# A second, transposed copy of x for the first norm, and a new order of the first loads, in a two-block transformer kernel on one Trainium2 core

## The reference

```
def rmsnorm(x, g):
    xf = x.astype(jnp.float32)
    y = xf * lax.rsqrt(jnp.mean(xf * xf, axis=-1, keepdims=True) + EPS)
    return (y * g.astype(jnp.float32)).astype(x.dtype)
```

## Time and profile before

| what | value |
|---|---|
| median of 3 runs | 866.22 us (866.06 to 866.31) |
| span of the profiled execution | 864.7 us |
| around it, to the median | 1.5 us |
| TensorE busy | 856.5 us, 99% of the span |
| VectorE, ScalarE busy | 604.2 us (70%), 501.3 us (58%) |
| HBM read | 152.53 MB |

### The profile page before, as it was taken

The page is one execution under the profiler, slowest core; times in us unless marked ns, Lnnn a source line. Parts: engine busy times, 40 slices in busy tenths (PEclk is TensorE's granted clock), DMA queues, the critical chain, the costliest instruction groups (busy, mean ns, idle before and its releaser), DMA issues.

```text
span 864.7 us, 12203 instructions
## 1 busy us (share of the span) xinstructions
PE 856.5 (99%) x4654; PEld 733.2 (85%) x4654; DVE 604.2 (70%) x1068; ACT 501.3 (58%) x873; POOL 36.1 (4%) x49
## 2 busy tenths in 40 slices
PE   9999999999999999999999999999999999999996
PEld 8998888888889999978888788888888888888885
DVE  6986666655767885779687466788458566777584
ACT  6435545446655676968678457654535456766540
POOL 0000000000010000000000001100020000000002
PEclk9999999999999999999999999999999999999999
DMA  9864544652583877543332457573764555434421
GB/s 326 280 222 166 195 149 144 207 194 98 195 268 128 285 241 233 148 147 98 127 119 97 146 194 225 191 269 126 265 202 153 182 195 192 150 120 172 165 79 49
DMA packets 86808, 154.36 MB, mean 179 GB/s; under 512 B 3744, under 2 KB 24352, under 8 KB 86752
## 3 DMA queue, kind: packets, MB, share of 16 engines
q1 hardware_dynamic: 85248, 149.19, 51.3%
q0 software_dynamic: 1360, 4.33, 1.7%
q10 hardware_dynamic: 144, 0.07, 0.0%
HBM read 152.53 MB, written 1.05 MB: 178 GB/s over the span
## 4 chain that ended last, share of the span: by engine, by line
PE 97%; DVE 1%; DMA 0%; ACT 0%; POOL 0%; issue 0%; DVEq 0%; POOLq 0%
PE acc L2273 11%; PE acc L2275 11%; PE acc L2274 11%; PE acc L2247 9%; PE acc L2249 9%; PE acc L2248 9%; PE acc L2291 5%; PE acc L2285 4%; PE acc L2286 4%; PE acc L2287 4%; PE acc L2292 3%; PE misc L2315 2%; PE misc L2445 2%; PE misc L2434 1%; PE acc L2305 1%; PE misc L2487 1%
## 5 line engine op out<-in xcount | busy, mean ns | idle before, releaser
L1455 DVE TENSOR_TENSOR wboth<-raw,wboth 128x1024 fp32r<-128x1024 f32 (+1 forms) x280 | 326.4, 1214 | 60.5 <-ACT wboth L973 59.0
L973 ACT ACTIVATE wboth<-raw 128x1024 fp32r<-128x1024 f32 (+1 forms) x280 | 278.9, 1052 | 122.9 <-PE acc L2275 67.4
L2273 PE MATMUL acc<-wboth,xhiA 128*128 128x512 f32 x272 | 107.8, 396 | 0.0
L2275 PE MATMUL acc<-wboth,xloA 128*128 128x512 f32 x272 | 106.1, 390 | 0.0
L2274 PE MATMUL acc<-wboth,xhiA 128*128 128x512 f32 x272 | 106.1, 390 | 0.0
L2247 PE MATMUL acc<-wboth,xhiA 128*128 128x512 f32 x240 | 93.9, 391 | 0.0
L2249 PE MATMUL acc<-wboth,xloA 128*128 128x512 f32 x240 | 93.5, 390 | 0.0
L2248 PE MATMUL acc<-wboth,xhiA 128*128 128x512 f32 x240 | 93.4, 389 | 0.0
L2291 PE MATMUL acc<-xC,wboth 128*128 128x512 f32 x192 | 68.7, 399 | 0.0
L2273 PEld LDWEIGHTS acc<-wboth,xhiA 128*128 128x128 f32 x272 | 51.1, 188 | 11.4 <-issue 1.2
L2275 PEld LDWEIGHTS acc<-wboth,xloA 128*128 128x128 f32 x272 | 51.0, 188 | 10.9
(11 more groups left out here) (335 smaller groups left out, 1721.0 us busy)
## 6 DMA issues: line engine op xcount, KB each, us to landing
raw<-in_w_in_dram SPq DMA_DIRECT2D x36, 1024.0 KB, 5.2
raw<-in_ret_w_in_dram SPq DMA_DIRECT2D x22, 1024.0 KB, 5.6
raw<-in_nsa_w_in_dram SPq DMA_DIRECT2D x16, 1024.0 KB, 5.5
raw<-in_kv_w_dram SPq DMA_DIRECT2D x12, 1024.0 KB, 6.7
raw<-in_ret_w_out_dram SPq DMA_DIRECT2D x8, 1024.0 KB, 5.1
raw<-in_ple_w_gate_dram SPq DMA_DIRECT2D x8, 1024.0 KB, 5.1
raw<-in_nsa_w_out_dram SPq DMA_DIRECT2D x8, 1024.0 KB, 5.1
raw<-in_cmp_w_k_dram SPq DMA_DIRECT2D x4, 1024.0 KB, 5.5
```

Source lines behind the costliest of these rows:

```text
L973: nc.scalar.activation(to_hi, src, ACT.Copy).then_inc(hi_done, 1)
L1455: nc.vector.tensor_tensor(to_lo, src, to_hi.bitcast(F32), ALU.subtract).then_inc(lo_done, 1)
L2273: nc.tensor.matmul(o, xh, hi[:, j, off:off + cols], start=start, stop=False)
L2275: ins = nc.tensor.matmul(o, xl, hi[:, j, off:off + cols], start=False, stop=stop)
```

## The change

x is handed in a second time as `x_T`, of shape 128 x 8 x 256 (column within the k-tile, k-tile, row), arranged on the host. It is loaded in four pieces, k-tiles 0, 1, 2 to 3 and 4 to 7, the second by SP behind chunk 0 and the others by ScalarE's queue; it lies in a part of the arena that was empty. ScalarE and VectorE read it there, in place of PSUM. The transposes go. `head` is loaded in two parts, the gains behind the first piece of x_T, and the identity last. The rows of x, which the squares and the residual sums still need, are loaded by SP behind chunk 4 and ahead of chunk 5. ScalarE squares all four pieces ahead of its high half of chunk 5, VectorE makes the low half of chunk 5 ahead of both sums, and the product `roots` stands behind all of chunk 5 instead of in its middle.

```
+XT_CUTS = (0, 1, 2, 4, 8)
...
-    norm("ret")
     r("ret_q0")
-    plan.half("ret_k0", 0, 0)
+    r("ret_k0", [0])
     m("roots")
-    plan.half("ret_k0", 0, 1)
     r("ret_k0", [1])
...
+        x_T = k3("x_T", 2048, KD)
...
+        def xT_part(i):
+
+            return x_T[:, XT_CUTS[i]:XT_CUTS[i + 1]], w["x_T"][:, XT_CUTS[i]:XT_CUTS[i + 1]]
+
+        def xT_wait(eng, k):
+
+            if k in XT_CUTS:
+                eng.wait_ge(xT_in[XT_CUTS.index(k)], 16)
...
         def _(sp):
-            for m in range(MT):
-                sp.dma_start(h[:, m], w["x"][0, m * P:m * P + P]).then_inc(x_in[m], 16)
             for c, (key, src, ks, width, *_) in enumerate(plan.chunks):
...
+                if c == 5:
+                    for m in range(MT):
+                        sp.dma_start(h[:, m], w["x"][0, m * P:m * P + P]).then_inc(x_in[m], 16)
                 sp.dma_start(raw_part(c).rearrange("p (k n) -> p k n", n=width), src).then_inc(raw_sem(c), 16)
+                if c == 0:
+                    sp.dma_start(*xT_part(1)).then_inc(xT_in[1], 16)
...
             def first_norm_hi():
 
+                act.wait_ge(ret_gain_in, 16)
                 for k in range(KD):
-                    misc_wait(act, "norm", "ret", k % 4)
-                    if k >= 4:
-
-                        act.wait_ge(operand_ready, xt_no["norm", "ret", k - 4] + 1)
-                    nc.scalar.activation(xhi["A"][:, k], first_columns(k), ACT.Copy, scale=cv["ret"][:, k:k + 1])                        .then_inc(operand_hi_done, 1)
+                    xT_wait(act, k)
+                    nc.scalar.activation(xhi["A"][:, k], x_T[:, k], ACT.Copy, scale=cv["ret"][:, k:k + 1])\
+                        .then_inc(operand_hi_done, 1)
...
-            act.dma_start(head[:], w["head"]).then_inc(head_in, 16)
+            act.dma_start(*xT_part(0)).then_inc(xT_in[0], 16)
+            act.dma_start(head[:, P:], w["head"][:, P:]).then_inc(ret_gain_in, 16)
             act.wait_ge(warm_set, 1)
             nc.scalar.activation(ssq[:, 0, 0:1], gains[:, 0, 0:1], ACT.Copy)
-            act.wait_ge(head_in, 16)
+            act.dma_start(*xT_part(2)).then_inc(xT_in[2], 16)
+            act.dma_start(*xT_part(3)).then_inc(xT_in[3], 16)
+            act.dma_start(head[:, 0:P], w["head"][:, 0:P]).then_inc(head_in, 16)
             first_norm_hi()
             for m in range(MT):
                 act.wait_ge(x_in[m], 16)
                 for nb in range(2):
                     square(m, nb)
-                split_until(len(FIRST_CUTS) + m)
+            split_until(len(FIRST_CUTS) + 1)
...
             first_norm_lo()
+            split_until(len(FIRST_CUTS))
             norm_stats("ret", 0)
-            split_until(len(FIRST_CUTS))
             asked = norm_stats("ret", 1)
 
             dve.wait_ge(*asked)
+            dve.wait_ge(head_in, 16)
...
                 elif kind == "roots":
 
+                    pe.wait_ge(head_in, 16)
                     pe.wait_ge(roots_spread, 1)
...
+    args["x_T"] = give("x_T", _np.ascontiguousarray(
+        _np.asarray(inputs["x"])[0].reshape(T, KD, P).transpose(2, 1, 0)))
```

More of the change, by code:

```diff
@@ L577, in build @@
         ret_kT = k3("ret_kT", 2048, 8)
-        here[0] += 2048
+        x_T = k3("x_T", 2048, KD)
         sTd = [carve(f"sTd{i}", 384) for i in range(2)]
@@ L673, in build @@
         head_in = sem("head_in")
+        ret_gain_in = sem("ret_gain_in")
+        xT_in = [sem(f"xT_in{i}") for i in range(len(XT_CUTS) - 1)]
         trig_in = sem("trig_in")
@@ L809, in build @@
         ones = gains[:, 0, 0:P]
-        def first_columns(k):
-            at_ = k // 4 * T
-            return bank("norm", "ret", k % 4)[:, at_:at_ + T]
+        def xT_part(i):
[3 more added lines that the diff above has]
+                eng.wait_ge(xT_in[XT_CUTS.index(k)], 16)
         def scores_of(hd, mp, qt):
@@ L1501, in first_norm_lo @@
                     dve.wait_ge(operand_hi_done, xts[0])
-                    freed[("norm", "ret", k % 4)] = xt_on(nc.vector.scalar_tensor_tensor(
-                        out=xlo["A"][:, k], in0=first_columns(k),
+                    xt_on(nc.vector.scalar_tensor_tensor(
+                        out=xlo["A"][:, k], in0=x_T[:, k],
                         scalar=cv["ret"][:, k:k + 1], in1=xhi["A"][:, k].bitcast(F32), op0=ALU.mult, op1=ALU.subtract))
@@ L2327, in misc @@
                     j = name[2]
[L2328 to L2338, removed]
-                    else:
[L2340 to L2344, removed]
-                            pe.wait_ge(residual_piece, 4 * (NORMS.index(name[1]) - 1) + MT * (1 + j // 2))
-                            parts = [(h[:, m, k * P:k * P + P], P) for k in (2 * j, 2 * j + 1) for m in range(MT)]
-                        ins = transposes(ps, parts)
+                    if name[1] == "kv":
+                        m, k0 = divmod(KD // 2 * j, KD)
+                        pe.wait_ge(rows_normed, m + 1)
+                        parts = [(xn_kv[:, m, k * P:k * P + P], P) for k in range(k0, k0 + KD // 2)]
+                    else:
+                        pe.wait_ge(residual_piece, 4 * (NORMS.index(name[1]) - 1) + MT * (1 + j // 2))
+                        parts = [(h[:, m, k * P:k * P + P], P) for k in (2 * j, 2 * j + 1) for m in range(MT)]
+                    ins = transposes(ps, parts)
                 elif kind == "roots":
+                    pe.wait_ge(head_in, 16)
                     pe.wait_ge(roots_spread, 1)
```

## The result

| | before | after |
|---|---|---|
| median | 866.27 us (866.06 to 866.59, 6 runs) | 869.15 us (868.52 to 869.98, 6 runs) |
| span of the profiled execution | 864.7 us | 867.0 us |
| start of `ret_q0`, first product | 8.09 | 6.37 |
| start of `ret_k0` | 19.70 | 20.72 |
| start of `ret_q1` | 31.64 | 33.85 |

The account below looks back on a forecast made before the run. TensorE, busy 99% of the span, bounds the kernel. The 2.3 us won in front go to waiting for chunk 5 (`ret_k0` at 19.6); plus 13.03, `ret_q1` starts at 32.63 against 31.46: +1.2, so 867.4 us, range 865.7 to 868.7.

Parts of the forecast that it names:

- The first wait: TensorE ahead of `ret_k0`: idle 1 to 1.5 us for VectorE's low half of chunk 5, spending the 2.3 us won.
- The first product: Start of `ret_q0`: without transposes it begins at 5.75, 2.3 us earlier, with x_T and gains landing at 4.7.
- The megabyte of part 2: Loads ahead of chunk 5: x_T adds 1.049 MB, 2.66 us at 394 GB/s, so chunk 5 lands at 17.2, not 14.5.
- A wait for x_T against weights may add some tenths: Products of `ret_q0`: x_T and weights share the DMA engines, which may delay its end by some tenths.
- S: Start of `ret_k0`: forecast 19.6 against 19.70 before, with a range from 18.6 to 20.7.
- part 3: Roots behind chunk 5: `ret_q1` starts at S + 13.03, where TensorE alone would be ready at S + 11.76; wait 1.27 us.
- The squares: ScalarE ahead of chunk 5: four squares, 2.9 us in all, cost nothing, covered with about 1 us to spare.
- Rival B, the clock: `ret_q0` without transposes: the clock rises late; a rise at 13 gives S = 20.9 and 868.7 us; chance 0.12.
- Rival D: Ahead of `ret_q1`: the roots wait does not decide, S = 19.6, start at 31.36, 866.1 us; chance 0.08.
- Rivals C and E: Front: C, chunk 5 isn't late, 865.9 us, chance 0.16; E, neither wait binds, clock high at once, 863.8, chance 0.05.

Follow-up runs that it names:

- d1: Changed kernel with the last piece of x_T issued by SyncE behind chunk 2 instead of by ScalarE ahead of it; 869.35 us, ratio 1.0034.
- p2: Changed kernel with the four x_T pieces as arrays of their own, all issued by SyncE ahead of their chunks; 868.96 us, ratio 1.0032.
- b1: Kernel before plus x_T loaded in one 1 MB transfer ahead of chunk 5, read by nothing; 866.49 us, ratio 1.0001.
- w1: Changed kernel with six ones products ahead of `ret_q0` in place of four; 869.64 us, ratio 1.0038.
- r1: Changed kernel with the product `roots` back in the middle of chunk 5's products; 868.41 us, ratio 1.0025.
- e1: Changed kernel with x_T loaded by SyncE in one transfer of 8 KB rows ahead of chunk 0; 869.37 us, ratio 1.0030.
- e3: e1 with eight ones products instead of four and nothing else changed; 867.27 us, ratio 1.0012.
- r2: Kernel before with only the product `roots` moved behind all of chunk 5's products; 867.44 us, ratio 1.0013.
- p1: Changed kernel with each of the four x_T pieces as its own array in HBM, same order and queues; 868.52 us, ratio 1.0026.
- q1: Changed kernel with all four x_T pieces issued by SyncE, each ahead of its chunk, instead of three by ScalarE; 869.90 us, ratio 1.0040.
- b3: Kernel before with x loaded in four 256 KB transfers of 2 KB runs instead of two of 512 KB; 867.53 us, ratio 1.0016.
- x1: Changed kernel with the rows of x loaded behind chunk 5 and squared behind its high half; 869.10 us, ratio 1.0031.
- x2: Changed kernel with both load orders altered, x1 and d1 together; 867.57 us, ratio 1.0014.

## Why the prediction was wrong

**Sign and mechanism, half right.** I forecast that the gain in front would be spent waiting for chunk 5, and that the roots would add a wait; the likeliest time was slower by 1.2 us. Both waits are there. Measured is 2.9, and the range ended at 868.7. The first wait does not show as idle time in after: TensorE was still in `ret_q0`, held back by the low clock until 12.5, when chunk 5's low half became ready, and the 1 to 1.5 us of idleness that I forecast ahead of `ret_k0` appear only in d1 (1.34) and p2 (1.41).

**The first product**: forecast 5.75, measured 6.37. ScalarE waited for the gains until 5.29, not 4.7; by my own bounds (4.3 to 5.1) this was late by 0.2. It had no consequence.

**The megabyte of part 2** is the step that failed. I put x_T at 394 GB/s, the rate of 9 to 14 us, and gave the start of the transfers half a microsecond in the bound only. b1 shows that 2.66 us is right for this megabyte in one transfer; cut in pieces of 1, 2 and 4 KB runs and placed first, it slowed all transfers between 2 and 7 us to 249 GB/s, and chunk 5 landed at 18.3, 3.8 us later than before and at the far end of my range. "A wait for x_T against weights may add some tenths" was the same error at chunk 2: it was 1.6 us in w1. By the sum of part 3, S = 20.72 instead of 19.6 gives 20.72 + 13.03 = 33.75, and measured is 33.85.

**The squares** ("cost nothing, covered by chunk 5's own transfer with about 1 us to spare") were a second term that failed. They took 3.0 us, about the 2.9 forecast, but chunk 2, late, kept ScalarE from them until 15.17, and they ended 0.1 us before chunk 5 was taken. With chunk 5 alone in time at 17.2, S would by these rows still have been near 20.6 (an estimate: 18.2 + 1.1 + 1.2 + 0.1), and no run tests that order by itself.

**Rival B, the clock**, had 0.12. In the profiled execution it came true: with the start at 6.37 and a rise at 12.5, 6.1/0.21 = 29 products are done at the low clock and the other 67 take 8.0 us, which ends at 20.5 to 20.6 against 20.7. (The low pitch is 0.21, not the 0.24 that I had taken as twice 0.12.) But w1 shows that with a high clock the start stays at 20.98, so it was one more bound at the same place and not the cause of the loss. Its late rise was one execution's: in r1, with the same front and loads, the products are fast from about 9 on. e1 and e3 show that it is a bound of its own, worth 2.1 us, once the transfers are in time. I had priced B and the late chunk as alternatives; they lay beside each other, so that mending one showed nothing.

**Part 3, the roots**: 13.03 us forecast, 13.03 in r2, 13.13 in after, with a wait of 1.1. Right in mechanism, and worth 1.1 us by itself in r2. The forecast wait was 1.27, because I put TensorE alone at 11.76 behind S, and the trace of before has 11.94; the same 0.18 made my shift of `ret_q1` 1.2 where my own terms give 1.0. Rival D falls.

**Rivals C and E** fall: chunk 5 was not early, and no version with the earlier first product ended earlier than the kernel before.

**The execution.** Some 0.6 of the 2.9 us are not in the spans compared: the profiled execution of after is 0.36 faster than its median, and the span of before was set against a median 0.3 too low for it. With 33.75 for `ret_q1`, against 31.64, the forecast would have been 868.3, inside the range, and 868.9 with this. So the miss of the range needed both. The executions of the kernel with late transfers also spread more, 868.5 to 870.0 against 866.1 to 866.6.

## What to carry to other kernels

At the start of a kernel the rate of a later stage is no price for the first transfers: take full rows in few transfers, or arrays cut as they are read, and look at the rate of the first microseconds by itself. Follow a late input through the work that its engine does before the next one: chunk 2, late by over a microsecond, held up the squares as well. When several things become ready at about the same time, price the second and the third as well: two experiments that each give nothing can give 1.6 us together. When a product that others wait for is moved back in one engine's order, count what the waiting engine does behind it until it releases the first: here one small product, moved back by 24 others, cost 1.1 us.

## What the runs showed that I had not expected

- The form of the first transfers: 249 GB/s from 2 to 7 us for runs of 1 to 4 KB out of rows of 8 KB, 300 for the same runs from arrays of their own, 345 for full rows (after, p1, e1).
- The clock fell to its lower level behind an idle stretch of 2.3 us (q1), also in the midst of transposes with a gap of 1.7 (b3), but not behind one of 2.0 (p2).
- The moment at which the clock rose differed between kernels with the same start of TensorE: about 12.5 in after and 13.5 in e1, whose TensorE paused from 5.0 on, 9 to 10 in r1, p1 and x1, and ahead of the first product in d1 and x2 (from 6.3), which had paused as well; there the first four take 0.74 us. A pause makes a late rise possible, not certain.
